# A weight pair as two transfers, of 120 and of 8 partitions, in a decoder trunk that gathers expert rows

## The reference, cut to what matters

```python
def retrieve(hb):                                   # hb: (tokens, 1024)
    q = (hb @ wq).reshape(chunk, 8, 2, 128)
    s = jnp.einsum('nhcd,hckd->nhck', q, sk)
    sv, si = lax.top_k(s, 16)
    cand = (sv[:, :, 0, :, None] + sv[:, :, 1, None, :]).reshape(chunk, 8, 256)
    cs, ci = lax.top_k(cand, 16)
    expert = i1 * 128 + i2                          # i1, i2 from si and ci
    g = jax.nn.softmax(cs, axis=-1)
    act = jax.nn.gelu(jnp.einsum('nd,nhkd->nhk', hb, u_tab[expert]))
    return jnp.einsum('nhk,nhkd->nd', (g * act), v_tab[expert])
```

## Time and profile before

| | |
|---|---|
| median of 3 runs | 3008.63 us (3007.17 to 3009.83) |
| the profiled execution | 3011.34 us; its span 3009.4 us |
| TensorE matmul busy | 2609.7 us, 87% |
| VectorE busy | 2108.1 us, 70% |
| ScalarE busy | 1285.6 us, 43% |
| GpSimd busy | 1206.2 us, 40% |
| moved by DMA | 1214.93 MB, mean 404 GB/s |
| granted TensorE clock | 0.979 of full speed |

### The profile page before, as it was taken

The page is one execution under the profiler, slowest core; times in us unless marked ns, Lnnn a source line. Parts: engine busy times, 40 slices in busy tenths (PEclk is TensorE's granted clock), DMA queues, the critical chain, the costliest instruction groups (busy, mean ns, idle before and its releaser), DMA issues.

```text
span 3009.4 us, 27506 instructions
## 1 busy us (share of the span) xinstructions
PE 2609.7 (87%) x7369; PEld 1282.4 (43%) x7369; DVE 2108.1 (70%) x5150; ACT 1285.6 (43%) x3706; POOL 1206.2 (40%) x1104
## 2 busy tenths in 40 slices
PE   8989999999988888888899889887899977777777
PEld 6675565555544443333444434333444422222222
DVE  3546766788766667777667677778676766777666
ACT  2123444655444434444443444345443444444444
POOL 2103443444444444444443444444343434334442
PEclk9999999999999999999999999999999999999999
DMA  9979999999999999999999999999999999999997
GB/s 346 334 280 366 382 421 410 417 395 411 422 421 421 421 421 413 421 422 394 422 421 419 381 421 416 421 422 412 421 416 419 410 421 406 420 422 410 420 414 319
DMA packets 175000, 1214.93 MB, mean 404 GB/s; under 512 B 19730, under 2 KB 20766, under 8 KB 33269
## 3 DMA queue, kind: packets, MB, share of 16 engines
q0 software_dynamic: 155904, 1124.11, 91.0%
q1 hardware_dynamic: 18941, 89.07, 7.6%
HBM read 1208.47 MB, written 38.37 MB: 414 GB/s over the span
## 4 chain that ended last, share of the span: by engine, by line
DMA 45%; PE 37%; DVE 8%; ACT 6%; issue 3%; POOL 1%; another core or an unknown queue 0%; DVEq 0%; SPq 0%; ACTq 0%; POOLq 0%
DMA RING<-in_peer_uv,idx 44%; PE PSUM L1291 22%; PE PSUM L974 10%; DVE RING L1998 5%; ACT diag L1489 2%; PE PSUM L985 1%; ACT L1480 1%; ACT gate L1485 1%; PE PSUM L956 1%; ACT act_h L1480 1%; PE PSUM L1279 1%; POOL RING L922 1%; ACT L1468 1%; DMA RING<-in_peer_uv,pidx 1%; PE PSUM L995 0%
## 5 line engine op out<-in xcount | busy, mean ns | idle before, releaser
L1291 PE MATMUL PSUM<-RING,diag 128*128 128x512 f32 (+1 forms) x4096 | 1977.2, 619 | 364.4 <-ACT diag L1489 358.0
L922 POOL DMA_INDIRECT RING<-in_peer_uv,idx x1024 | 1155.8, 1129 | 1593.5 <-PE PSUM L1291 1481.2
L1998 DVE CUSTOM_DVE_ANT_0 RING<-RING,H 128x1024 f32<-128x1024 f32 x1032 | 1263.5, 1225 | 650.2 <-DMA RING<-in_peer_uv,idx 636.1
L1291 PEld LDWEIGHTS PSUM<-RING,diag 128*128 128x128 f32 (+1 forms) x4096 | 737.9, 192 | 1446.0 <-ACT diag L1489 820.3
L1480 ACT ACTIVATE act_h<-dots 128x1 f32<-128x1 f32 x1040 | 208.2, 200 | 1112.5 <-DVE dots L1998 1110.8
L1489 ACT ACTIVATE diag<-ident,gate 128x128 f32<-128x128 f32 x1008 | 404.8, 402 | 33.1 <-PE PSUM L1291 0.3
L974 PE MATMUL PSUM<-HT,WCH 128*128 128x256 f32 (+2 forms) x1408 | 335.0, 385 | 1.5 <-ACT HT L1344 1.3
L1485 ACT ACTIVATE gate<-act_h,ex 128x1 f32<-128x1 f32 x1008 | 296.8, 294 | 32.7
L974 PEld LDWEIGHTS PSUM<-HT,WCH 128*128 128x128 f32 x1408 | 265.3, 192 | 90.9 <-issue 59.2
L1480 ACT ACT_TABLE_LOAD x91 | 116.8, 1283 | 6.9 <-DVE dots L1998 5.3
L1344 ACT ACTIVATE YT<-PSUM 128x256 f32<-128x256 f32 (+4 forms) x70 | 27.4, 391 | 191.4 <-PE PSUM L974 166.8
(11 more groups left out here) (265 smaller groups left out, 1523.8 us busy)
## 6 DMA issues: line engine op xcount, KB each, us to landing
WCH<-in_peer_wq SPq DMA_DIRECT2D x28, 1024.0 KB
WCH<-in_w_in_ab SPq DMA_DIRECT2D x18, 1024.0 KB
RING<-in_peer_uv,idx POOLq DMA_INDIRECT x1024
out_win_k_sample<-in_state_win_k POOLq DMA_DIRECT2D x8, 2016.0 KB, 12.6
out_win_v_sample<-in_state_win_v POOLq DMA_DIRECT2D x8, 2016.0 KB, 12.0
RING<-in_w_in_ab SPq DMA_DIRECT2D x6, 1024.0 KB, 14.4
WCH<-in_w_out_ab SPq DMA_DIRECT2D x6, 1024.0 KB
X<-in_x_prompt SPq DMA_DIRECT2D x4, 512.0 KB, 9.4
```

Of the source, the lines that this page charges most:

```text
L922: pool.indirect_dma_start(rows[:, use % SLOTS, :], None, peer_uv.rearrange("l e n -> (l e) n"), bass.IndirectOffsetOnAxis(ap=at, axis=0),) ...
L1291: last = nc.tensor.matmul(PSUM[0:out_n, accumulator(n) + half, :], diag[:, at % DIAGS, 0:out_n], rows[:, use % SLOTS, D + half * 512:D + h ...
L1998: V.tensor_tensor_reduce(out=u, in0=u, in1=row, scale=1.0, scalar=0.0, op0=ALU.mult, op1=ALU.add, accum_out=dots[:, tau % SETS, k:k + 1]). ...
```

## The change

A pair that is sent beside the gathers goes out as two transfers, one of partitions 0 to 119 and one of partitions 120 to 127. Both add 16 to the home's semaphore, and the readers' counts are worked out from the number of transfers into the home so far (`loads_by`). Pairs sent earlier go as one transfer as before. The set of split pairs has kinds "p", "v" and "wo" of the second half, "q" of layer 0's second half and all "q" of layer 1: 40 of 64.

```diff
+BESIDE_GATHERS = [(kind, 1) for kind in ("p", "v", "wo")] + [("q", 1)]
+
+
+def load_parts(n):
+
+    if beside_gathers(n):
+        return (0, 120), (120, P)
+    return (0, P),
+
+
+def beside_gathers(n):
+    piece = chunk_list()[2 * n]
+    return piece[0:2] in BESIDE_GATHERS or piece[0:3] == ("q", 0, 1)
...
+        PARTS = [load_parts(n) for n in range(len(HOMES))]
+
+        def loads_by(n):
+            return sum(len(PARTS[m]) for m in range(n + 1) if HOMES[m][0] == HOMES[n][0])
...
         def wait_pair(eng, piece):
             home, use = HOMES[CHUNKS.index(piece) // 2]
-            eng.wait_ge(w_loaded[home], 16 * (use + 1))
+            eng.wait_ge(w_loaded[home], 16 * loads_by(CHUNKS.index(piece) // 2))
             return pair_buffer(home)
...
-            eng.wait_ge(w_loaded[home], 16 * (use + 1) if home < NW_FIRST + 3 else 32)
+            eng.wait_ge(w_loaded[home], 16 * loads_by(n) if home < NW_FIRST + 3 else 32)
...
-                    sp.dma_start(pair_buffer(home), src).then_inc(w_loaded[home], 16)
+                    for lo, hi in PARTS[n]:
+                        sp.dma_start(pair_buffer(home)[lo:hi, :, :, :], src[lo:hi, :, :, :]).then_inc(w_loaded[home], 16)
```

## The result

The changed kernel takes 3196.76 us (median of 4, 3192.48 to 3200.32) beside 3007.9 for the kernel before (its three runs and a fourth): ratio 1.063, 95% interval 1.0611 to 1.0649. It is 189 us slower, 4.7 us for each of the 40 pairs. The profiled execution has a span of 3194.3 us.

What follows compares the result with a forecast made beforehand. It took gathers in flight on the DMA queues to bound the kernel after 840 us, TensorE before; -15.4 - 1.4 + 4.1 + 0.6 = -12.1 us from 3008.63 gave 2996.5 us, range 2974 to 3014.

Steps and rivals of the forecast that it cites:

- What bounds the kernel: From 840 us on gathers in flight, 46.8 to 70.1% of the chain; between 320 and 840 us TensorE.
- (b) to (d): For the 40 pairs: relieving one engine gains 15.4 us after 840 us, extra rows on eight cost 4.1 us.
- R1: Slower, chance 0.19: beside loads, the late engine is among the eight with extra rows; 3014 to 3021 us.
- (c): Relieving one DMA engine of its rows gains 15.4 us after 840 us and 1.4 us before.
- R3: Full gain, chance 0.12: the relieved engine is the late one, its head start carries through stretches without loads; 2977 us.
- The front part: Before 840 us transfers are 11.4% of the chain, so a gain of 1.4 us and a cost of 0.6.
- R2: No change, chance 0.19: the 16 DMA queues are loaded alike or 120 rows are divided alike; 3006 to 3011 us.
- (e): SP's issue per pair grows from 328 to at most 1360 ns, 1.03 us more; effect on the time zero.
- (f): Wait for both transfers of a pair: tightest turn 16.8 us against 16.0 needed; zero, up to 2 us.

Runs made afterwards that it cites:

- Without pairs: Changed kernel with the 40 pairs beside the gathers not sent at all, products using older weights: 2941.15 us, ratio 0.9771 to the kernel before.
- 32 to 95: Changed kernel with only partitions 32 to 95 of each of the 40 pairs sent: 2961.95 us, ratio 0.987 to the kernel before.
- 15 rows: Kernel before plus two extra HBM-to-HBM transfers of 15 rows beside each of the 40 whole pairs: 3024.77 us, ratio 1.0073; with 16 rows 3027.5 us.
- the probe: Kernel before plus two extra HBM-to-HBM transfers beside each of the 40 whole pairs; with 8 rows each: 3013.09 us, ratio 1.0033.

## Why the prediction was wrong, point by point

**What bounds the kernel** was right. Without pairs 67 us are saved, some 14 of them before 840 us, where TensorE keeps the pace.

**The step that failed is the price of a split, (b) to (d).** I priced a split by the rows that each engine carries, 0.31 us a pair, with 0 and 12.4 us as ends. Rows an engine is one cost; where the engines' rows lie is another, and it wasn't in the sum. A split pair measured 4.4 us by the rates and 4.7 by the times, fifteen times the term. The sentence "nothing in the rows shows a port limit" was wrong twice. The Trainium skill's rule against splits stood beside it, and I gave it R1's price in place of one of its own. (As worded there, that only 128 partitions reach all ports, it is too strict: 32 to 95 ran at the full 421 GB/s.) And the trace did hold a hint of a price: the one 120-partition transfer of the kernel before, HT<-in_state_pool, 480 KB at 1688.4 us, whose issue is the first of the earlier trace rows. The window over its flight:

```profile
1688.40:1704.70 16.30, 12.80 (x36) 5.64 (x34) 8.52 (x23) 5.17 (x19) 7.49 (x7) 1.00 1.00 354
```

354 GB/s with a share of 1.00, where whole pairs go at 421: 16.3 x (1 - 354/421) = 2.6 us at most, for less than half a pair's bytes (a whole pair flies beside it). It isn't a clean figure, since the rate just before was low too, there with pauses of the engines (a share of 0.96). The end of the flight is the plainer sign; the rate comes back when the transfer has landed:

```profile
1662.00:1678.00 16.00, 13.86 (x43) 7.26 (x44) 10.78 (x23) 10.03 (x30) 4.21 (x5) 1.00 0.96 357
...
1700.00:1704.70 4.70, 1.99 (x4) 0.68 (x4) 1.81 (x4) 0.90 (x3) 1.71 (x2) 1.00 1.00 323
1704.70:1710.00 5.30, 4.01 (x6) 1.67 (x7) 4.08 (x13) 1.84 (x7) 0.84 (x1) 0.71 1.01 420
```

Forty times 2.6 us are over 100 us. I took the issue time of this transfer and not the rate around it.

**(c), the relief**, failed too. If the dealing is as assumed, the engine left out isn't the late one (15 rows cost what 16 cost), and no head start shows where no loads are (372.5 against 373.0 us for 148 gathers). Whether one engine is overloaded at all stays open. The gain of the forecast and of R3 would most likely not have come even without the placement loss.

**The front part.** I costed it at 0.11 of anything, since TensorE sets the pace. The cover was 5% thick: 493.73 us busy of 520, with transfers at 412 GB/s right behind. Costs of 0.3 us a pair hide under that, 4.4 don't: 188 gathers became 161. Counted from the first, the 220th gather is issued at 839.3 us in before and at 919.4 in after, with 18 split pairs sent by then: 80 of the 189 us.

```profile
L922 POOL DMA_INDIRECT RING<-in_peer_uv,idx x220: 932/947/1956, 223.6 to 839.3; - x110
```

```profile
L943 POOL DMA_INDIRECT RING<-in_peer_uv,idx x220: 932/940/1987, 218.8 to 919.4; - x110
```

**R1** had the sign and the place (longer flights where loads are), not the mechanism: twice 8 rows a pair in the probe cost 9 us, so no extra row on the first eight explains 189. **R2** fell with the result. Two ends of the range don't follow from their sums: R3 gives 2977, not 2974, and R1 with its front part hidden 3008.6 + 6.8 = 3015, not 3014. Neither matters beside 3197.

**(e)** SP's issues take 324 and 305 ns (first and second of the pair at 1594.9 us), not 735 and 625. What makes those of the earlier trace rows longer is open. Nothing waits for SP either way.

```profile
L757 SPq DMA_DIRECT2D WCH<-in_peer_wq x2: 305/314/324, 1594.9 to 1595.3; - x2
```

**(f)** was right in its zero: no wait for a pair stands among the waits of after. Its margin was misread. The turn of 16.8 us isn't the tightest; behind the load at 448.1 us the next goes out after 13.7, less than the 16.0 that it was held against (and 759.7 to 773.5 is as short). What covers it is that a whole pair is quicker than the 14.6 us taken for it, 9.2 us to landing in the median, as the page of the run with 15 rows has it.

```profile
L736 SPq DMA_DIRECT2D WCH<-in_w_in_ab x2: 328/328/328, 448.1 to 461.8; - x2
...
WCH<-in_peer_wq SPq DMA_DIRECT2D x28, 1024.0 KB, 9.2
```

What grew are the waits for gathers, 841.7 us of DVE's in place of 636.1:

```profile
DVE RING L2019 <- DMA RING<-in_peer_uv,idx: 841.7, 791, 7.5
```

## What to carry to other kernels

A transfer beside a saturated stream is priced by the rate of the whole core while it flies, not by its bytes or its engines: ask the windows around each transfer of that shape that the trace already holds. Keep weight loads on all 128 partitions and split them by columns if they must be split; in these runs, 64 partitions at the full rate were those from 32 to 95. Before an engine is relieved, find out that it is the late one, with a small dose on some engines and not on others.

## What the runs showed of the hardware that was not expected

The busy share of the DMA engines stays at 1.00 to 1.02 while the rate falls from 421 to 290 GB/s; only GB/s tells the two apart. And TensorE's granted clock fell, to 0.951 over the span from 0.979. TensorE's timeline in after (start us, us, what, idle before it and who ended it) shows how it goes beside the load at 1594.9 us, then VectorE's wait for the gather whose gate TensorE needs, and three windows: TensorE's wait and what follows:

```profile
1589.56 3.60 PE L1312 MATMUL PSUM<-RING,diag 128*128 128x512 f32 x8
...
1609.38 6.33 PE L1312 MATMUL PSUM<-RING,diag 128*128 128x512 f32 x8 [5.11 <-ACT diag L1510]
...
1607.09 1.23 DVE L2019 CUSTOM_DVE_ANT_0 RING<-RING,H 128x1024 f32<-128x1024 f32 x1 [6.50 <-DMA RING<-in_peer_uv,idx]
...
1604.30:1609.40 5.10, 0.02 (x1) 0.03 (x1) 2.10 (x7) 0.90 (x3) 0.94 (x1) 0.81 1.02 247
1609.40:1612.30 2.90, 2.90 (x4) 1.15 (x4) 1.42 (x3) 0.15 (x1) 0.00 (x0) 0.50 1.02 418
1615.70:1620.90 5.20, 5.20 (x17) 2.80 (x16) 3.81 (x10) 2.28 (x8) 2.42 (x2) 1.00 1.01 422
```

VectorE waits 6.50 us for a gather, and TensorE 5.11 for the diagonal made from its product. Eight matmuls take 3.60 us before that wait and 6.33 after it. Right behind the wait the granted clock is 0.50, the lower of its two levels (1.2 GHz), and from 1615.7 on it is 1.00 again. Over the span the same 7369 matmuls kept TensorE busy for 2676.8 us in place of 2609.7. How much of the 189 us this adds wasn't tried.
